# A projection that begins while its input is still being turned

## The reference

```python
proj = jnp.einsum("bsd,de->bse", x, w_in)                  # w_in: 1024 x (4*1024 + 16)
q, k, v, gate = jnp.split(proj[..., :4 * ATTN_WIDTH], 4, axis=-1)
f_logit = proj[..., 4 * ATTN_WIDTH:] + b_f                 # 16 forget logits per position
cum = jnp.cumsum(jax.nn.log_sigmoid(f_logit), axis=1)      # one running sum per head
```

## Time and profile before

| | us |
|---|---|
| median of 3 runs | 2590.55 (2588.41 to 2590.64) |
| the profiled execution | 2593.75 |
| its span in the trace | 2591.9 |
| PE busy | 2417.6 |
| DVE busy | 1339.5 |
| ACT busy | 1156.4 |
| GpSimd busy | 623.0 |
| last evacuation of the projection begins | 772.78 |

### The profile page before, as it was taken

The page is one execution under the profiler, slowest core; times in us unless marked ns, Lnnn a source line. Parts: engine busy times, 40 slices in busy tenths (PEclk is TensorE's granted clock), DMA queues, the critical chain, the costliest instruction groups (busy, mean ns, idle before and its releaser), DMA issues. The chain is left out here.

```text
span 2591.9 us, 41884 instructions
## 1 busy us (share of the span) xinstructions
PE 2417.6 (93%) x13921; PEld 2086.2 (80%) x13921; DVE 1339.5 (52%) x2832; ACT 1156.4 (45%) x2128; POOL 623.0 (24%) x740
## 2 busy tenths in 40 slices
PE   8899999999997999999999999599689999993898
PEld 7688889998876888898888988488578888872786
DVE  4312121211007888888888888433245666574333
ACT  4211111111116888888888888400034556575000
POOL 0000000000002555455545555234300000000244
PEclk9999999999998999999999999799899999996999
DMA  5344343332116445544454444545344354435553
GB/s 182 112 114 130 114 128 107 123 113 86 52 49 146 98 97 126 128 97 96 111 128 111 96 98 95 181 159 194 122 147 122 127 158 130 138 123 168 195 191 135
DMA packets 215772, 325.65 MB, mean 126 GB/s; under 512 B 16097, under 2 KB 141089, under 8 KB 209441
## 3 DMA queue, kind: packets, MB, share of 16 engines
q1 hardware_dynamic: 215136, 323.68, 43.4%
q0 software_dynamic: 512, 0.53, 0.1%
HBM read 197.79 MB, written 126.35 MB: 125 GB/s over the span
## 5 line engine op out<-in xcount | busy, mean ns | idle before, releaser
L760 DVE TENSOR_TENSOR at_pl<-at_tps,at_ph 128x512 fp32r<-128x512 f32 (+3 forms) x640 | 371.0, 604 | 21.7 <-ACT at_ph L705 21.5
L705 ACT ACTIVATE at_ph<-at_tps 128x512 fp32r<-128x512 f32 (+3 forms) x640 | 312.3, 528 | 108.6 <-PE at_tps L627 104.7
L323 ACT ACTIVATE pa_stg<-pa_ps 128x512 fp32r<-128x512 f32 (+1 forms) x128 | 76.2, 597 | 608.1 <-PE pa_ps L227 608.1
L627 PE MATMUL at_tps<-at_ident,at_probs 128*128 128x128 f32 x2176 | 338.3, 273 | 1.4 <-DVE at_pl L760 1.4
L642 PE MATMUL at_ops<-at_ph,at_val 128*128 128x256 f32 (+1 forms) x1152 | 325.1, 304 | 2.0 <-DVE at_pl L760 1.9
L227 PE MATMUL pa_ps<-pa_xh,pa_wh 128*128 128x512 f32 x800 | 312.9, 391 | 12.1 <-DVE pa_stg L390 9.6
L695 ACT ACTIVATE at_probs<-at_probs,at_least 128x128 f32<-128x128 f32 (+15 forms) x256 | 307.1, 1200 | 18.9 <-DVE at_probs L751 18.8
L227 PE MATMUL pa_ps<-pa_xl,pa_wh 128*128 128x512 f32 x800 | 312.2, 390 | 0.0
L227 PE MATMUL pa_ps<-pa_xh,pa_wl 128*128 128x512 f32 x800 | 312.2, 390 | 0.0
L612 PE MATMUL at_sps<-at_k,at_q 128*128 128x512 f32 (+3 forms) x640 | 272.2, 425 | 26.1 <-DMA at_k<-forget_sums 22.1
L642 PE MATMUL at_ops<-at_pl,at_val 128*128 128x256 f32 (+1 forms) x1152 | 294.8, 281 | 0.0
(11 more groups left out here) (165 smaller groups left out, 4664.2 us busy)
## 6 DMA issues: line engine op xcount, KB each, us to landing
at_q<-q_halves SPq DMA_DIRECT2D x48, 512.0 KB
at_k<-k_halves SPq DMA_DIRECT2D x48, 512.0 KB
pa_wst<-in_attn_w_in SPq DMA_DIRECT2D x16, 1024.0 KB, 7.2
q_halves<-pa_stg SPq DMA_DIRECT2D x32, 512.0 KB, 3.7
k_halves<-pa_stg SPq DMA_DIRECT2D x32, 512.0 KB, 3.7
v_halves<-pa_stg SPq DMA_DIRECT2D x32, 512.0 KB, 2.8
at_val<-v_halves SPq DMA_DIRECT2D x16, 1024.0 KB, 16.8
ma_yin<-y_halves SPq DMA_DIRECT2D x8, 2048.0 KB, 9.0
```

The lines of the kernel that those rows point to most:

```text
L323: nc.scalar.activation(out, source(kind, s), func, scale=scale).then_inc(evac_h, 1)
L627: mm = nc.tensor.transpose(tps[c % TB][:, k, :], probs[s % ROWS][:, t0:t0 + P], ident[:, :])
L705: nc.scalar.activation(ph[g % 2][:, j * PB:j * PB + n, i % 2 * P:(i % 2 + 1) * P], tps[c % TB][:, 0:n, :], ACT.Copy).then_inc(high_out, 1)
L760: nc.vector.tensor_tensor(pl[g % 2][at], tps[c % TB][:, 0:n, :], raw(ph[g % 2][at]), ALU.subtract)\
```

## The change

In the first two strips (16 tiles, `EARLY`) the order changes from strip by strip to chunk by chunk: `place` maps tile number t to a strip and its place there. PE turns the four tiles of chunk 0, and then computes for each chunk its four tiles (two halves of 128 columns of strip 0, then two of strip 1), with the turns of the four x tiles of the next chunk put between them. The forget logits of all chunks stand behind tile 15, in the `tps` banks, with buffers of their own for their weights (`wf`, `wfs`); softplus and the sums follow behind the evacuations and low halves of tiles 16, 18, 20 and 22.

The first two strips are loaded and split in halves of 128 columns. `wst` is one buffer of 1 MB instead of two, so a strip is loaded when the one before it is split: on SP the load of strip s+1 stands ahead of the stores of strip s. The x tiles behind the first four are loaded into `fbuf` and `fsm` (three slots), since `stg` now holds outputs. The forget weights come behind all these loads. GpSimd fills `wf` with zeros once. Before a product, PE waits for the low half of the tile four before it only, for the gate strips too. The streams are written out in full, without `Fori`. With every change of order the semaphores' counts change.

```diff
+    EARLY = 2 * TILES
+    strips = [(kind, col + j * STRIP, j, dst, g) for g, (kind, col, n, dst) in enumerate(groups) for j in range(n)]
+    def place(t):
+        if t < EARLY:
+            c, b = t // 4, t % 4
+            return b // MT, b % MT * NS + c
+        return t // TILES, t % TILES
...
-        wst = a.sb("wst", [P, 2, KC, STRIP])
+        wst = a.sb("wst", [P, KC, STRIP])
+        wf = a.sb("wf", [P, 2, KC, P], F32R)
+        wfs = a.sb("wfs", [P, KC, HEADS])
...                                                      # SP
+            for t in range(4):
+                load_x(t)
+            for m in range(MT):
+                load_half(0, m)
+            for t in range(4, 7):
+                load_x(t)
+            for m in range(MT):
+                load_half(1, m)
+            sp.dma_start(wfs[:, :, :], w_v[:, :, 4 * D:4 * D + HEADS]).then_inc(f_in, 16)
+            sp.dma_start(bf[:, :], gate_bias.rearrange("(h a) -> h a", a=1)).then_inc(f_in, 16)
+            for c in range(NS):
+                for b in range(4):
+                    for t in {0: (7,), 1: (8,), 2: (9, 10), 3: ()}[b]:
+                        if 4 * c + t < ST:
+                            load_x(4 * c + t)
+                    store(4 * c + b)
+                if c == 1:
+                    load_strip(2)
+            for strip in range(2, LAST):
+                if strip + 1 < LAST:
+                    load_strip(strip + 1)
+                for q in range(TILES):
+                    store(strip * TILES + q)
...                                                      # PE
-                for n in range(NS):
-                    turn_chunk(n)
-                    if n:
-                        forget_logits(n - 1)
-                forget_logits(NS - 1)
...
+            for t in range(4):
+                turn(t)
+            for c in range(NS):
+                for b in range(4):
+                    if b == 3 and c + 1 < NS:
+                        turn(4 * c + 7)
+                    product(4 * c + b)
+                    if b < 3 and c + 1 < NS:
+                        turn(4 * c + 4 + b)
+            for n in range(NS):
+                forget_logits(n)
+            for t in range(EARLY, LAST * TILES):
+                product(t)
...                                                      # ACT: high() and evacuate() in PE's order, then
+            for t in range(EARLY, LAST * TILES):
+                evacuate(t)
+                if (t - EARLY) % 2 == 0 and t < EARLY + 2 * NS:
+                    softplus((t - EARLY) // 2)
...                                                      # DVE
+            for t in range(4):
+                low(t)
+            for m in range(MT):
+                split(0, m, 1)
+            for c in range(NS):
+                for b in range(4):
+                    if b == 3 and c + 1 < NS:
+                        low(4 * c + 7)
+                    take_low(4 * c + b)
+                    if b < 3 and c + 1 < NS:
+                        low(4 * c + 4 + b)
+                    if c == 0 and b < MT:
+                        split(1, b, 2)
+                    if c == 2 and b == 3:
+                        split_forget()
+                    if c + 1 == NS and b == 1:
+                        split(2, None, 3)
+            nc.vector.memset(fo, 0.0).then_inc(f_dve, 1)
+            for strip in range(2, LAST):
+                if strip + 1 < LAST:
+                    split(strip + 1, None, (strip + 1) // 2 + 2)
+                for q in range(TILES):
+                    take_low(strip * TILES + q)
+                    if strip == 2 and q % 2 == 0:
+                        forget_sums(q // 2)
```

More of the change, by code:

```diff
@@ L77, in project, with tile_done, split_in, low_count @@
     NS = S // BANK
-    TILES = 8
+    MT = STRIP // P
+    TILES = MT * NS
     RING = 4
+    EARLY = 2 * TILES
     w_v = w.rearrange("(c p) f -> p c f", p=P)
+    strips = [(kind, col + j * STRIP, j, dst, g) for g, (kind, col, n, dst) in enumerate(groups) for j in range(n)]
+    LAST = len(strips)
+    def place(t):
[3 more added lines that the diff above has]
+        return t // TILES, t % TILES
+    def tile_done(strip):
+        return EARLY - 2 + 2 * strip if strip < 2 else (strip + 1) * TILES
+    def split_in(kind):
+        return kind in ("split", "rows")
+    def low_count(t):
+        return sum(split_in(strips[place(k)[0]][0]) for k in range(t))
+    def piece(strip, m=MT - 1):
+        return 2 * strip + m + 1 if strip < 2 else strip + 3
     with ExitStack() as ctx:
@@ L142, in _ @@
[L142 to L184, removed]
@@ L185, in _, with load_x, load_half @@
-            if cum is not None:
-                sp.wait_ge(f_stored, 64 * NS)
+            def load_x(t):
+                if t >= 7:
+                    sp.wait_ge(x_turned, 2 * (t - 3) + 2)
+                sp.dma_start(slot(t), x[t * P:(t + 1) * P, :]).then_inc(slot_sem(t)[0], 16)
+            def load_half(strip, m):
+                col = strips[strip][1] + m * P
+                wait(sp, w_split, piece(strip - 1) if strip else 0)
+                sp.dma_start(wst[:, :, m * P:(m + 1) * P], w_v[:, :, col:col + P]).then_inc(w_loaded[m], 16)
@@ L285, in _, with high, evacuate @@
         def _(act):
-            act.sem_inc(high_out, 4)
+            def high(t):
+                for b in range(2):
+                    act.wait_ge(x_turned, 2 * t + b + 1)
+                    nc.scalar.activation(xh[:, 4 * b:4 * b + 4, t * P:(t + 1) * P], tps[(2 * t + b) % 4][:, :, :],
+                                         ACT.Copy).then_inc(high_out, 1)
+            def evacuate(t):
+                kind, _, _, _, g = strips[place(t)[0]]
+                func = ACT.Silu if kind == "silu" else ACT.Copy
+                scale = -HEAD_DIM ** -0.5 if kind == "split" and g == 0 else 1.0
+                s = t % RING
+                act.wait_ge(products, t + 1)
+                wait(act, stored[s], 16 * (t // RING))
+                out = halves(kind, s)[0] if split_in(kind) else raw(stg[:, s, 0, :])
+                nc.scalar.activation(out, source(kind, s), func, scale=scale).then_inc(evac_h, 1)
@@ L311, in _ @@
-            for s in range(RING):
-                act.sem_inc(stored[s], 16)
-            for g, (kind, col, n, dst) in enumerate(groups):
-                func = ACT.Silu if kind == "silu" else ACT.Copy
-                scale = -HEAD_DIM ** -0.5 if kind == "split" and g == 0 else 1.0
-                with act.Fori(0, n // 2) as i:
-                    for q in range(2 * TILES):
-                        t, s = (first_strip[g] + 2 * i) * TILES + q, q % RING
-                        act.wait_ge(products, t + 1 + 2 * TILES)
-                        uses = (first_strip[g] + 2 * i) * (TILES // RING) + q // RING
-                        act.wait_ge(stored[s], 16 * uses + 16)
-                        out = raw(stg[:, s, 0, :]) if kind in ("plain", "silu") else halves(kind, s)[0]
-                        nc.scalar.activation(out, source(kind, s), func, scale=scale).then_inc(evac_h, 1)
+            for t in range(4):
+                high(t)
@@ L326, in _, with low @@
         def _(dve):
[L327 to L329 removed]
+            def low(t):
+                for b in range(2):
+                    dve.wait_ge(high_out, 2 * t + b + 1)
+                    at = (slice(None), slice(4 * b, 4 * b + 4), slice(t * P, (t + 1) * P))
+                    nc.vector.tensor_tensor(xl[at], tps[(2 * t + b) % 4][:, :, :], raw(xh[at]), ALU.subtract)\
+                        .then_inc(low_out, 1)
@@ new lines, in split @@
+            def split(strip, m, loads):
+                u = strip % 2
+                n = piece(strip) if m is None else piece(strip, m)
+                cols = slice(0, STRIP) if m is None else slice(m * P, (m + 1) * P)
+                dve.wait_ge(w_loaded[u if m is None else m], 16 * loads)
+                if strip >= 2:
+                    dve.wait_ge(products, tile_done(strip - 2))
+                nc.vector.tensor_copy(wh[:, u, :, cols], wst[:, :, cols]).then_inc(w_high, 1)
+                dve.wait_ge(w_high, n)
+                nc.vector.tensor_tensor(wl[:, u, :, cols], wst[:, :, cols], raw(wh[:, u, :, cols]), ALU.subtract)\
+                    .then_inc(w_split, 1)
@@ new lines, in take_low @@
+            def take_low(t):
+                kind, _, _, _, g = strips[place(t)[0]]
+                if not split_in(kind):
+                    return
+                scale = -HEAD_DIM ** -0.5 if kind == "split" and g == 0 else 1.0
+                s = t % RING
+                dve.wait_ge(evac_h, t + 1)
+                hi, lo = halves(kind, s)
+                if scale != 1.0:
+                    nc.vector.scalar_tensor_tensor(out=lo, in0=source(kind, s), scalar=scale, in1=raw(hi),
+                                                   op0=ALU.mult, op1=ALU.subtract).then_inc(evac_l, 1)
+                else:
```

(1 more changed line is left out.)

283 lines of the change are left out of this document (121 added, 162 removed).

## The result

The changed kernel takes 2616.61 us (five runs, 2615.90 to 2617.29), the one before 2590.55 (2588.41 to 2592.20): a ratio of 1.0098, 95% interval 1.0087 to 1.0109. That is 26 us slower; 17.1 us faster was forecast. The profiled execution took 2615.9 us, span 2614.1.

A forecast was written before the change was run, and what follows sets the result against it. The projection was taken as PE-bound, with gains in PE's gaps and slow work. Terms to tile 16 gave -15.4, the gate strips -1.7: 17.1 us off 2590.55, so 2573.5 (range 2571 to 2576, chance 0.75).

The forecast's parts named there:

- Nothing else moves: The four stages behind the projection were to run unchanged, only beginning 17.1 us earlier.
- The backward jumps of the loops inside that stretch cost nothing: In the old projection, 47 tiles took 5.44 us each, so its loop jumps were read as free.
- Start of the first product: First product after turning chunk 0 and splitting the first weight piece: 14.7 against 13.97 before, +0.7 us.
- Turns: Turning chunks 1 to 3 between products: twelve turns of 0.88, 10.6 us instead of 14.5, -3.9 us.
- Clock: Half-rate clock at product 0 was to cost 1.8 us (bounds 1.1 to 2.4), against 2.8 before: -1.0 us.
- rival 1: Evacuations pace turns, product 0 runs 5 us at half rate, gate gap stays: gain 11.9, 2578.6; chance 0.16.
- Tile 16 evacuated: The end of projection tile 16, at 156.80 before, was to come near 141.5 us.
- The 9.56 us stall: PE's wait before tile 4, behind forget sums and strip 1's split, was to go whole: -9.6 us.
- Gate wait: Where v strips end and gate strips begin, PE's wait for all low halves was to go: -1.7 us.
- The single weight buffer: One strip buffer instead of two was to cost nothing, with 8 us of cover before PE would wait.
- Rival 2: Slow loads into the single weight buffer make PE wait at nine strip boundaries: 10 us lost, 2583.5; chance 0.02.
- Rivals 3 and 4: 3: half-clock spells at sixteen products, 2602. 4: an equal wait replaces the logits, 2590. Chance 0.02 each.

The follow-up runs named there:

- e9: e4 with the four softplus rounds and four forget sums put back to back again, as before the change: 2584.68 us, 11.3 over e4.
- e4: The changed kernel with PE's attention loop over the pairs written out instead of a hardware loop: 2573.43 us, ratio 0.9938.
- e11: The changed kernel with semaphore increments ahead of the attention's first score, shifting PE's attention loop by 8 instructions: 2576.5 us.
- e12: The changed kernel with PE's attention loop shifted by 24 instructions through semaphore increments; its single time is within 2573.4 to 2576.5 us.
- e13: The changed kernel with PE's attention loop shifted by 4 instructions through 5 semaphore increments: 2574.57 us (a single run).
- e6: The kernel before the change with PE's attention loop over the pairs written out: 2588.44 us, ratio 0.9993.
- e1: The changed kernel with 41 semaphore increments ahead of the first attention score, shifting PE's loop by 40 instructions; five runs spread over 8.3 us, median not given.
- e15: The changed kernel with PE's attention loop shifted by 88 instructions through semaphore increments; 50 instruction packets, time not given.
- e3: The changed kernel with 129 semaphore increments ahead of the first attention score, shifting PE's loop by 128 instructions: 2597.5 us.
- e5: The kernel before the change with 217 semaphore increments, shifting PE's attention loop by 216 instructions: some 36 us slower than that kernel on the same chip (2590.16).
- e7: The changed kernel with PE's attention loop shifted by 64 instructions through semaphore increments; 24 instruction packets, time not given.
- e8: The changed kernel with PE's attention loop shifted by 200 instructions through semaphore increments; padding shows as +14 us, total time not given.
- e14: The changed kernel with 249 semaphore increments, shifting PE's attention loop by 248 instructions; padding shows as +21 us, total time not given.

## Why the prediction was wrong

**The step that failed** is "Nothing else moves: the other four stages begin after the barrier, 17.1 us earlier." They do begin earlier, but the attention is not the same machine work: its loop's place in the program moved by 2 instructions modulo 256, the body came to span eight blocks, and six jumps cost 41.1 us. The prediction gave the other stages a term of nothing, without a look at what they share with the projection: PE's instruction stream. A second sentence fed that error: "The backward jumps of the loops inside that stretch cost nothing". That was read rightly of the projection, whose loop bodies are 788 to 1572 instructions. It was no evidence on a body of 1759 and on whether its place is safe. The row to ask about was the 14 packets of PE's instruction queue in the attention: it says that the body was kept from pass to pass. That seven blocks are the most that is kept, and that the loop was one instruction behind a block's edge, takes the runs above.

The Trainium skill, page "Runtime: NRT & Kernel Launch", section "Instruction fetch mechanics", bears on it: PE's instruction memory takes 2048 instructions in 16 KiB blocks of 256, and a taken branch out of the window that is held stalls on a fetch. The runs agree with the block's size, and with a memory of eight blocks if one of them is always being fetched ahead (that last is inferred). They don't agree with that section's window of two pages: before jumps back over seven blocks with 14 packets in all and no stall. By that window the loop would have stalled at each jump in both kernels, and the change would have made no difference there. None of the four rivals of the prediction was a stall at the jumps, which turned out to cost 6 x 6.9 us.

**The terms**, read from the timeline of ACT (evacuations) and the table of stretches of the kernel after:

```profile
22.17 0.60 ACT L323 ACTIVATE pa_stg<-pa_ps 128x512 fp32r<-128x512 f32 x1 [11.16 <-PE pa_ps L250]
28.51 0.60 ACT L323 ACTIVATE pa_stg<-pa_ps 128x512 fp32r<-128x512 f32 x1 [4.76 <-PE pa_ps L250]
...
141.76 0.60 ACT L323 ACTIVATE pa_stg<-pa_ps 128x512 fp32r<-128x512 f32 x1 [26.60 <-PE pa_ps L250]
```

```profile
13.97:19.90 5.93, 5.93 (x15) 0.56 0.67 203
13.97:21.98 8.01, 8.01 (x25) 0.68 0.74 196
21.98:28.31 6.33, 6.33 (x33) 1.00 0.58 166
```

- Start of the first product: 13.97 against 14.7 forecast. The last low half is done 0.7 us sooner than reckoned: PE's first turn began at 4.17 and not 4.63, since its x tile had landed sooner, which is luck, and the split of the forget weights (6.48 to 7.04 on DVE before) no longer stands ahead of the low halves.
- Turns: 28.51 - 22.17 - 5.44 = 0.90 each, forecast 0.88; -3.7 for the twelve against -3.9.
- Clock: product 0 took 8.01, 2.6 over 5.44 where 1.8 was taken; the bounds (1.1 to 2.4) were just left, and this part of rival 1 held. The row of the recurrent layer was the wrong model, since here PE stays near half rate for 5.93 us (0.56).
- Tile 16 evacuated at 141.76, forecast 141.5: the early start and the slow first product cancel, which is luck. The 9.56 us stall is gone. e9 prices one like it: 11.3 with its clock, against 9.6 + 1.0 of the sum.
- Gate wait: none, as forecast. The last evacuation is at 755.86 against 772.78, 16.9 sooner.
- The single weight buffer: DVE waits 13 times for weights, 164 us in all, and PE never for it. Rival 2 was rightly small.
- Rival 1: turns not paced and no gate gap, so only its slow first product held. Rivals 3 and 4: turns at 1.00, and a stage that is shorter. Neither held. (What rival 3 has from the Trainium skill, page "TensorE: Matmul & The Clock Gate", stands in its section "A second HAM failure mode: psum-queue depth-cycling", next to the one named; the stretch from 21.98 to 28.31, at 1.00, disagrees with it too.) "A stage end that is earlier while the total is not" was named as a sign of error, and it is what happened.

With the jumps harmless the changed kernel takes 2573.4 to 2576.5 us (e4, e11 to e13), where 2573.5 was forecast. Against the kernel before on the same chips that is 13 to 17 us less (e11 to e13, single runs, and e4), 15.0 by e4 and e6, and 16.9 in the stage itself, where 17.1 was forecast; on two of these three chips the kernel before ran about 1 us under the 2590.55 that the forecast counts from, so the near hit on 2573.5 is in part luck. The mechanism and roughly the size of the projection's gain are shown; what was missing is a term of another stage, +41.

**Open.** What decides whether a jump refetches with few instructions in the eighth block: 0 or 1 of 6 at 6 to 30 instructions, 4 of 6 at 54, all six from 94 on. That looks like a race between the fetch ahead and the jump, but nothing here shows when the ninth block is asked for. Why three of the stalls of e1 and e15 last 3.9 to 4.2 us, and the others there and at other offsets some 2.3, is not known. How each jump's cost splits between fetch and clock at other offsets was not separated either.

## What to carry to other kernels

When a change alters how many instructions an engine has ahead of a later hardware loop, that loop's place is part of the change: count the body and its start modulo 256, and look at the instruction queue's packets and at "issue" idle time at the first instruction of a pass. A body of PE of at most 1537 instructions (1 + 6 x 256) spans at most seven blocks anywhere, an estimate from the seven blocks of 256 that were kept here; a longer one should be placed, or written out, which cost nothing here (e6). A gain should be summed stage by stage in the trace before its total is believed or doubted.

## What the runs showed of the hardware that was not expected

- Four instructions ahead of a loop decide over 42 us: 2616.61 us at offset 255, 2574.57 at offset 3 (a single run).
- PE jumped back over seven blocks of 256 instructions without fetching any (14 packets), and at eight it fetched nine for each jump (67).
- A refetch stops PE for 1.9 to 2.8 us for the target's block in e3, e5, e7, e8 and e14 (up to 4.2 in e1 and e15), and for 2.1 to 2.8 more if the second is needed at once (e14); straight-line code costs none (e4, 52 packets).
- A bare semaphore increment on PE costs some 0.15 us: 249 of them brought the first score's wait from 22 to 43.3 us, 129 to 24.86.
